# Mixture-of-experts rows stored as whole rows from one gathered tile instead of straight from four partition strips

## The reference

```python
e = group * 8 + inner            # top-1 group of 4, then top-2 of 8 experts in it
for a block of rows xb of the tokens routed to expert e:
    y = (silu(xb @ w1[e]) * (xb @ w3[e])) @ w2[e]    # w1, w3: 1024 x 512; w2: 512 x 1024
out[token] += weight * y         # over a token's two experts
```

## Time and profile before

| | us |
|---|---|
| median of 3 runs | 2973.35 (2972.33 to 2974.61) |
| the profiled execution: its time | 2970.88 |
| its span, first to last instruction | 2969.1 |
| `experts` of layer 0, first matmul of `pg` to the copy of the last block | 731.4 to 1450.1 |
| `experts` of layer 1, the same | 2269.0 to 2877.3 |

### The profile page before, as it was taken

The page is one execution under the profiler, slowest core; times in us unless marked ns, Lnnn a source line. Parts: engine busy times, 40 slices in busy tenths (PEclk is TensorE's granted clock), DMA queues, the critical chain, the costliest instruction groups (busy, mean ns, idle before and its releaser), DMA issues. The chain is left out here.

```text
span 2969.1 us, 61155 instructions
## 1 busy us (share of the span) xinstructions
PE 2285.1 (77%) x24807; PEld 1533.9 (52%) x24808; DVE 1103.9 (37%) x1927; ACT 696.2 (23%) x1470; POOL 415.5 (14%) x600
## 2 busy tenths in 40 slices
PE   5887862993989898869469989886974887778970
PEld 3676641872544454434258857675762444444430
DVE  4689997663111111101164013285651110111105
ACT  4211012540111111101143124485320111111112
POOL 0000001001111111111121100253001111111114
PEclk9889885995999999979789999898987998989985
DMA  8365332228778976992264210045549999999916
GB/s 306 106 221 168 118 128 74 93 100 352 303 312 318 377 297 237 359 397 102 100 222 147 77 54 22 31 162 203 201 152 401 399 351 368 348 360 355 331 55 223
DMA packets 243071, 662.84 MB, mean 223 GB/s; under 512 B 24025, under 2 KB 77225, under 8 KB 242947
## 3 DMA queue, kind: packets, MB, share of 16 engines
q1 hardware_dynamic: 195740, 575.59, 52.3%
q0 software_dynamic: 19280, 56.60, 5.4%
q10 hardware_dynamic: 27928, 28.95, 2.9%
HBM read 583.52 MB, written 77.55 MB: 223 GB/s over the span
## 5 line engine op out<-in xcount | busy, mean ns | idle before, releaser
L1361 PE MATMUL moe_pg<-feed_w,moe_xt 128*32 128x256 f32 x11200 | 699.6, 405 | 180.0 <-SPq L1307 169.7
L1361 PEld LDWEIGHTS moe_pg<-feed_w,moe_xt 128*32 128x32 f32 x11200 | 364.8, 116 | 454.9 <-SPq L1307 175.1
L1460 DVE TENSOR_TENSOR moe_a<-moe_sil,moe_pg 128x128 f32<-128x128 f32 x175 | 50.6, 289 | 807.7 <-ACT moe_sil L1424 807.7
L1354 PE MATMUL moe_py<-feed_w,moe_at 128*32 128x256 f32 x5536 | 334.6, 382 | 0.0
L1424 ACT ACTIVATE moe_sil<-moe_pg 128x128 f32<-128x128 f32 x175 | 48.6, 278 | 834.8 <-PE moe_pg L1361 834.8
L1322 POOL COPY moe_idx<-plan_token 128x1 int32 (+1 forms) x183 | 33.5, 183 | 1371.1 <-DVE moe_x_rows L1452 974.9
L1354 PEld LDWEIGHTS moe_py<-feed_w,moe_at 128*32 128x32 f32 x5536 | 161.4, 109 | 110.7
L1325 POOL DMA_INDIRECT moe_xg<-scratch_experts_in,moe_idx x183 | 178.7, 976 | 144.4 <-POOL moe_idx L1322 143.2
L1462 DVE COPY moe_at<-moe_pat 128x128 f32<-128x128 f32 x175 | 51.1, 292 | 334.3 <-PE moe_pat L1376 334.3
L1432 ACT ACTIVATE moe_y<-moe_py 128x256 f32<-128x256 f32 x173 | 66.6, 385 | 275.3 <-PE moe_py L1354 275.3
L103 PE MATMUL taps_zg<-ht_conv_hi,taps_w_hi 128*128 128x512 f32 (+1 forms) x192 | 77.5, 404 | 66.7 <-DVE taps_w_lo L548 51.1
(11 more groups left out here) (336 smaller groups left out, 3802.7 us busy)
## 6 DMA issues: line engine op xcount, KB each, us to landing
feed_w<-in_moe_w SPq DMA_DIRECT2D x384, 1024.0 KB, 14.6
taps_ada_w<-in_ada_w SPq DMA_DIRECT2D x40, 1024.0 KB, 7.0
scratch_experts_out<-moe_y ACTq DMA_DIRECT2D x173, 128.0 KB
taps_raw<-in_conv_pw_w SPq DMA_DIRECT2D x20, 512.0 KB, 9.2
scan_v<-scratch_gla_values SPq DMA_DIRECT2D x20, 512.0 KB, 3.8
front_w<-in_ada_w SPq DMA_DIRECT2D x8, 1024.0 KB, 18.0
cv_raw<-in_gla_w_in SPq DMA_DIRECT2D x16, 512.0 KB, 5.0
scratch_gla_out<-scan_o SPq DMA_DIRECT2D x16, 512.0 KB, 6.5
```

Of the source, the lines that this page charges most:

```text
L1354: last = pe.matmul(out[j * BLK:(j + 1) * BLK, 0:CUT], at[:, c * BLK:(c + 1) * BLK], feed.back[:, buf, c, j * CUT:(j + 1) * CUT], start=c = ...
L1361: last = pe.matmul(pg[j * BLK:(j + 1) * BLK, 0:2 * P].rearrange("t (m n) -> t m n", m=2), xt[:, c % 2, (c // 2) * BLK:(c // 2 + 1) * BLK], ...
```

## The change

The four buffers `y[b]` of 128 partitions x 256 become one tile of 128 partitions x 1024, in which buffer b is partitions 32b to 32b+31: a whole row of the block lies in one partition. So `py` is taken in four copies, each of one strip of 32 partitions x 256, into the four column ranges of the same 32 partitions: ACT takes strips 0 and 1 (`y_near`), DVE strips 2 and 3 (`y_far`). ACT then waits for both counts, signals `y_out`, and issues the store: 32 rows of 1024 numbers. `y_last` is gone; the last block uses buffer 0.

```diff
-        y = [ph.sb(f"y{p}", [P, CUT]) for p in range(UNROLL)]
-        y_last = ph.sb("y_last", [P, CUT])
+        ys = ph.sb("y", [P, D])
+        y = [ys[p * BLK:(p + 1) * BLK, :] for p in range(UNROLL)]
...
-                def store(k, src, stored):
-                    act.dma_start(d.yd[ds(k * BLK, BLK), :].rearrange("t (s n) -> s t n", n=CUT), src).then_inc(s(stored), 16)
+                def take_y(b, src):
+                    for j in range(2):
+                        act.activation(y[b][:, j * CUT:(j + 1) * CUT], src[j * BLK:(j + 1) * BLK, 0:CUT], ACT.Copy)\
+                            .then_inc(s("y_near"), 1)
+
+                def store(k, b, stored):
+                    act.wait_ge(s("y_near"), k * 2 + 2)
+                    act.wait_ge(s("y_far"), k * 2 + 2)
+                    act.sem_inc(s("y_out"), 1)
+                    act.dma_start(d.yd[ds(k * BLK, BLK), :], y[b]).then_inc(s(stored), 16)
...
-                        act.activation(y[b][:, :], py[:, 0:CUT], ACT.Copy).then_inc(s("y_out"), 1)
-                        act.wait_ge(s("y_out"), k + 1)
-                        store(k - 1, y[b][:, :], f"y_stored{b}")
+                        take_y(b, py)
+                        store(k - 1, b, f"y_stored{b}")
...
+                def take_y(b, src):
+                    for j in range(2, STRIPS):
+                        dve.tensor_copy(y[b][:, j * CUT:(j + 1) * CUT], src[j * BLK:(j + 1) * BLK, 0:CUT]).then_inc(s("y_far"), 1)
...
                     dve.tensor_tensor(a[:, :], sil[:, :], pg[:, P:2 * P], ALU.mult).then_inc(s("a_ready"), 1)
+                    if started(k, 1):
+                        b = (p - 1) % UNROLL
+                        dve.wait_ge(s("back_done"), k)
+                        if started(k, UNROLL + 1):
+
+                            dve.wait_ge(s(f"y_stored{b}"), (i - (1 if p == 0 else 0)) * 16)
+                        take_y(b, py)
                     dve.wait_ge(s("at_turned"), k + 1)
                     dve.tensor_copy(at[:, :], pat[:, 0:P]).then_inc(s("at_ready"), 1)
```

More of the change, by code:

```diff
@@ L1336, in finish @@
                         pool.wait_ge(s(f"y_stored{p}"), ((last + (UNROLL - 1 - p)) >> 2) * 16)
-                    pool.wait_ge(s("y_last_stored"), 16)
+                    pool.wait_ge(s("last_stored"), 16)
                 for k in range(UNROLL):
@@ L1431, in body @@
                             act.wait_ge(s(f"y_stored{b}"), (i - (1 if p == 0 else 0)) * 16)
-                        act.activation(y[b][:, :], py[:, 0:CUT], ACT.Copy).then_inc(s("y_out"), 1)
-                        act.wait_ge(s("y_out"), k + 1)
-                        store(k - 1, y[b][:, :], f"y_stored{b}")
+                        take_y(b, py)
+                        store(k - 1, b, f"y_stored{b}")
                 def tail(count, last):
                     act.wait_ge(s("back_done"), count)
-                    act.activation(y_last[:, :], py_last[:, 0:CUT], ACT.Copy).then_inc(s("y_out"), 1)
-                    act.wait_ge(s("y_out"), count + 1)
-                    store(last, y_last[:, :], "y_last_stored")
+                    act.wait_ge(s("y_stored0"), ((last + (UNROLL - 1)) >> 2) * 16)
+                    take_y(0, py_last)
+                    store(last, 0, "last_stored")
                 take_x(0)
@@ L1460, in body, with tail @@
                     dve.tensor_tensor(a[:, :], sil[:, :], pg[:, P:2 * P], ALU.mult).then_inc(s("a_ready"), 1)
+                    if started(k, 1):
[4 more added lines that the diff above has]
+                        take_y(b, py)
                     dve.wait_ge(s("at_turned"), k + 1)
                     dve.tensor_copy(at[:, :], pat[:, 0:P]).then_inc(s("at_ready"), 1)
+                def tail(count, last):
+                    dve.wait_ge(s("back_done"), count)
+                    dve.wait_ge(s("y_stored0"), ((last + (UNROLL - 1)) >> 2) * 16)
+                    take_y(0, py_last)
                 bring_x(0, 0, 0)
-                blocks(dve, body)
+                blocks(dve, body, tail)
         ph.sems.update(feed.sems)
```

## The result

The changed kernel takes 2883.95 us (median of 4 runs, 2878.01 to 2884.77) against 2972.84 (2970.64 to 2974.61): a ratio of 0.9697, 95% interval 0.968 to 0.9714. That is 89 us less, where 112 were forecast. The profiled execution took 2883.63 us, 87.3 less than that of before.

The account below looks back on a forecast made before the run. The weight stream, slowed by stores on four DMA engines, was taken to bound experts with few blocks. Layer 1's 70 us plus layer 0's 42 gave 112 off 2970.88: 2859, or 2861 for the median; range 2820 to 2905.

Parts of the forecast that it names:

- The bound and the store: Where PE starves, the weight stream ends last; each store goes from 1.47 us on four engines to 0.32 on 16.
- Layer 1: 70 forecast: Layer 1's experts, nearly all starved: 2.5 us less each, from 19.5 to 16.9 us, for 28 experts, 70 us.
- The "28": In layer 1, some 28 of 32 experts are loaded behind running stores, each gaining 2.5 us.
- Layer 0: 42 forecast: Layer 0's runs of short experts, where the stream is late: 42 us gained, low bound 30, high bound 51.
- they have about 9, 8, 9, 9 and 12 stores: Stores in layer 0's five stretches with PE idle, at 1.15 us each and capped by idle time: in sum 51 us.
- a sixth: Taken off layer 0's 51 us, giving 42, because each run begins with full buffers and its first stores delay nothing.
- The copies: Four copies per block on ACT and DVE, 0.4 us each, hidden by the next `in_product`: costed at nothing.
- Half speed: Stores from 32 partitions cost 0.64 us on 16 engines, gaining 0.83 per block: 2893 us; chance 0.14.
- Another cause of layer 1's rate: Layer 1's low rate comes from mixed reads and writes, weight placement, or a still-split store: 9 us at most, 2964; chance 0.09.
- the twelve engines: Loads end last on the engines without stores, so spreading adds 0.32 us per store: 36 us more, 3009; chance 0.04.
- The late handover: Copies over 1.5 us push `x_rows` on DVE past PE's need; at 2.25 us a copy, +60, 3033; chance 0.03.
- more than the sum: All PE waits for weights go, and clock losses with them: 150 us gained, 2821; chance 0.08.

Follow-up runs that it names:

- Experiments 1 to 3: Kernel before, store split into four strip DMAs: 2883.72 us; kernel after, layer 1's whole-row stores on four engines: 2949.53; on eight: 2903.01.
- experiments 8 and 9: PE waits for the loads' own completion counts instead of SP's signals: kernel before so changed 2934.60 us, kernel after 2838.97.
- direct waits: PE waits on the weights' own completion counts, not SP's signals pair_ready and back_ready: 2934.60 us on the kernel before, 2838.97 on the kernel after.
- experiments 4 and 5: Layer 1's stores, all but the last, and their waits left out: kernel before 2886.89 us, kernel after 2863.62.
- experiment 8: PE waits for the loads' own completion counts instead of SP's signals; on the kernel after 2838.97 us, ratio 0.9542.

## Why the prediction was right, and where its sizes were off

**The bound and the store: right.** The forecast was 112 us and the change gave 89, with the bound and the cause as forecast and both terms too large. The rate, the 16 small packets, the full share and the unchanged block came as named. The store's price, 1.47 to 0.32 us, measured 1.47 to 0.34. Experiments 1 to 3 show that the spread alone does it: the gain comes with strips on 16 engines and goes with whole rows on four. How much of layer 1's time hangs on the spread:

| layer 1 of | us per block on the engines used | layer 1, us |
|---|---|---|
| no stores (after) | 0 | 525.5 |
| after | 0.34 on 16 | 542.9 |
| whole rows on eight | 0.64 on 8 (5.1/8) | 562.9 |
| before | 1.47 on 4 | 603.6 |
| whole rows on four | 1.28 on 4 | 610.4 |

**Layer 1: 70 forecast, 60.7 measured.** The part per expert was right, or nearly: between 2400 and 2700 us 111.61 MB of weights came in 300 us, an expert in 16.9 us, as worked out. The "28" was too high. Stretches of the kernel before, then of the kernel after (columns as in the earlier trace rows):

```profile
2269.00:2350.00 81.00, 75.17 (x1139) 40.26 (x1143) 9.63 (x34) 11.78 (x34) 13.90 (x24) 0.93 1.02 403
2350.00:2810.00 460.00, 377.49 (x5684) 200.07 (x5676) 50.52 (x173) 60.04 (x172) 66.18 (x115) 0.91 1.00 357
...
2330.00:2730.00 400.00, 364.47 (x5659) 196.22 (x5654) 92.85 (x285) 75.44 (x228) 65.12 (x112) 0.95 1.03 408
```

In the first 81 us of layer 1 the old stores ran too, some 10 of them (1297 packets of queue q10 at 132 each), and the rate was 403 GB/s all the same. It fell only from about 2350 us on. In the 460 us that follow, 149.39 MB of weights came, 23.8 experts at 19.4 us. In the 400 us of the kernel after 148.22 MB came, at 17.0 us an expert. So 24 experts gained 2.4 us each, 57 us, and that is nearly all of the 60.7. It also accounts for most of "about two thirds": some 57 of the 79 blocks lie in such a stretch (ACT's 172 and 228 entries over three and four). This is worked out from the two traces; no run varied it.

PE's waits for SP fell less than named, to 40.2 us and not 15 to 35, and in layer 0 to 61.3 and not some 45. Here SP's late signals have their part, by experiments 8 and 9. That the change is worth 70.7 in layer 1 without them, almost the 70 of the forecast, is luck. In the kernel before with direct waits the rate falls from 2320 us on, and it is then lower than in the kernel before: 348 GB/s from 2320 to 2800, with 151.00 MB of weights, 20.0 us an expert. With direct waits the kernel after has 17.0 (147.56 MB from 2300 to 2700). That is 24 experts at nearly 3 us and not 28 at 2.5. Why the old stores delay the loads more there stays open.

**Layer 0: 42 forecast, 26.7 measured.** The step "they have about 9, 8, 9, 9 and 12 stores" at 1.15 us each failed. I counted ACT's entries in stretches of 65 to 130 us. Each took in blocks in which PE no longer waited, and one run lies in none of the five (923.5 to 961.9 us). The runs proper are found by PE's starts at experts 0, 4, 8, 12, 16 and 20. Three of the six in the kernel before (columns as in the earlier trace rows):

```profile
839.80:874.30 34.50, 22.64 (x301) 11.29 (x297) 2.62 (x9) 3.14 (x9) 4.14 (x7) 0.85 1.03 410
...
999.00:1039.30 40.30, 28.51 (x400) 14.74 (x396) 3.49 (x12) 4.18 (x12) 5.01 (x9) 0.85 1.03 414
...
1194.00:1359.50 165.50, 119.24 (x1691) 61.50 (x1687) 14.90 (x51) 17.79 (x51) 19.63 (x35) 0.82 0.92 362
```

And the same three in the kernel after:

```profile
841.70:875.90 34.20, 23.33 (x302) 11.47 (x298) 4.88 (x15) 4.12 (x12) 4.47 (x7) 0.80 1.02 409
...
994.60:1028.40 33.80, 26.84 (x400) 14.17 (x396) 6.51 (x20) 5.41 (x16) 5.63 (x9) 0.91 1.03 413
...
1179.10:1334.20 155.10, 116.68 (x1691) 60.70 (x1687) 27.69 (x85) 22.96 (x68) 19.76 (x34) 0.87 0.97 387
```

These gain 0.3, 6.5 and 10.4 us; the other three (735.7, 923.5 and 1089.2 us in the kernel before) 0.1, 5.9 and 3.7. The sum is 26.9, the whole of layer 0. The runs hold some 4, 3, 5, 4, 4 and 17 blocks (ACT's entries before, over three), 30 in the last four. At 1.13 us the 30 are 34 us; with the two thirds that reach the time in layer 1 they would be 23. That is near the 26.9, but it doesn't hold run by run. The first two runs gained 0.4 us with 7 blocks, the next three 5.9, 6.5 and 3.7 us with 5, 4 and 4 blocks (at 1.13 us: 5.6, 4.5 and 4.5), and the last 10.4 us with 17 (19). The run that the forecast passed over gave 5.9, so its own five gave 21.0 of the 42. So a fixed price per store is wrong in layer 0. The rate of a run doesn't tell either: the run at 839.8 had 410 GB/s before and gained nothing, the one at 999.0 had 414, no less than after, and gained 6.5. So here the store can delay PE without lowering the rate. Why the first two runs lost nothing, I only argue: few stores stand beside a queue of several loads, as the forecast said when it took off a sixth. The sixth was too little, and what sets the price of a store in each run stays open.

**The copies: right.** They show no cost in experiments 4 and 5. PE came to wait longer for `at` only before `py_last`, 1.2 us in each layer instead of 0.4. No `in_product` hides the copies there.

**The rivals.** Half speed came for a store that runs alone (0.58 us) and not beside the loads (0.34 and 0.33), which is where it would count. The Trainium skill, "SBUF — State Buffer", section "Door 1: The DMA port swizzle (why `[64,N]` ≈ `[32,N]`)", has 189 GB/s for 32 partitions, measured at 1 MiB, and about 218 as the limit for large transfers. The lone store, of 128 KB, came to 226 GB/s over its 0.58 us and to 281 in its best slice, so it is near that limit and far below the 408 of the earlier trace rows. Beside the loads the trace shows no half rate. Another cause of layer 1's rate is out by experiments 1 to 3; the twelve engines, too, since more work on them went with a higher rate. The late handover and "more than the sum" did not come; with PE's waits changed as in experiment 8 the time is 2839. The sum of the handover rival was wrong in itself: its 88 blocks that are not starved don't go with the 47 + 67 starved ones that the forecast has elsewhere, which leave 61 of 175.

## What to carry to other kernels

When a stream of loads sets the pace, count the engines that each small store beside it uses (the small packets of one that runs alone) and give it an outer dimension that spreads it over all of them, as 32 rows did: here four engines more heavily used than the other twelve cost 89 of 2973 us, and splitting the DMA in four was as good as rebuilding the tile. When a gain is summed over runs of short work, bound the runs by the waiting engine's own starts, and don't multiply one price per transfer over all of them: in layer 1 the old stores ran for 81 us at 403 GB/s before the rate fell, and in layer 0 the gain per block went from nearly nothing to 1.6 us (6.5 us over four). Let an engine wait for a load's own semaphore where the one that issues can be held in issuing: that gave 45 us more.

## What was not expected of the hardware

A lone store from 32 partitions holds each of 16 engines 0.58 us, beside loads 0.34. In layer 1 the old stores ran beside the loads for 81 us at 403 GB/s before the rate fell, and some runs of layer 0 kept 410 to 414 GB/s throughout. ACT's time in issuing a store fell with the pattern; tile `y`'s stores before, then after (shortest, median, longest, in ns):

```profile
L1417 ACTq DMA_DIRECT2D scratch_experts_out<-moe_y x173: 544/555/1129, 748.4 to 2871.1; - x173
```

```profile
L1425 ACTq DMA_DIRECT2D scratch_experts_out<-moe_y x175: 321/322/398, 750.9 to 2791.8; - x175
```

It is 555 ns for 4x32x256 and 322 for 32x1024. And in the profiled executions the whole rows on four engines cost more than the strips on four (67.5 against 60.7 us over the kernel after) though their packets take less time. No run here tells why, and it stays open.
